# Skewing the attention bias with a repeated table in HBM instead of flip matmuls

## The reference

```
dist = qi + W - kj
bias = jnp.moveaxis(rel_bias[t5_bucket(dist * r)], -1, 0)
s = jnp.einsum('bnqchd,bnkchd->bnchqk', qb, kb).astype(jnp.float32) * (dh ** -0.5)
s = s + bias.astype(jnp.float32)
s = jnp.where(valid[None, :, None, None], s, -jnp.inf)
```

## Time and profile before

| | |
|---|---|
| median of three runs | 1124.41 us (1123.78 to 1126.25) |
| the profiled execution, its own time | 1126.25 us |
| its span, first to last instruction | 1124.4 us |
| TensorE matmul busy | 1025.4 us, 91% |
| VectorE busy | 859.4 us, 76% |
| ScalarE busy | 619.6 us, 55% |
| mean granted TensorE clock | 0.948 of full speed |

### The profile page before, as it was taken

The page is one execution under the profiler, slowest core; times in us unless marked ns, Lnnn a source line. Parts: engine busy times, 40 slices in busy tenths (PEclk is TensorE's granted clock), DMA queues, the critical chain, the costliest instruction groups (busy, mean ns, idle before and its releaser), DMA issues.

```text
span 1124.4 us, 13500 instructions
## 1 busy us (share of the span) xinstructions
PE 1025.4 (91%) x4842; PEld 851.0 (76%) x4842; DVE 859.4 (76%) x928; ACT 619.6 (55%) x535; POOL 95.9 (9%) x77
## 2 busy tenths in 40 slices
PE   4999999999999994789999999999999999999740
PEld 3788797978768784678888888888888888888630
DVE  3387838383855676679989999899999999999738
ACT  3223515153354233357777777777777777777622
POOL 3100000000000031000111101111011110111014
PEclk8999999999989995789999999999999999999965
DMA  9432212122132645479999999999999999999141
GB/s 287 116 105 76 75 38 75 38 76 75 75 112 75 230 177 231 166 278 356 367 367 363 361 381 368 359 357 374 380 373 360 356 376 370 384 365 346 39 174 75
DMA packets 71649, 268.67 MB, mean 239 GB/s; under 512 B 7412, under 2 KB 28920, under 8 KB 53696
## 3 DMA queue, kind: packets, MB, share of 16 engines
q1 hardware_dynamic: 64352, 252.72, 60.0%
q0 software_dynamic: 7264, 15.51, 3.9%
HBM read 264.83 MB, written 13.13 MB: 247 GB/s over the span
## 4 chain that ended last, share of the span: by engine, by line
PE 84%; DVE 8%; DMA 3%; ACT 3%; issue 2%; SPq 0%; DVEq 0%; POOLq 0%; ACTq 0%
PE ps L778 34%; PE ps L802 17%; PE ps L520 9%; PE ps L521 8%; PE ps L522 8%; PE ps L763 1%; PE ps L753 1%; DMA raw_m<-in_w_in 1%; PE ps L813 1%; PE ps L545 1%; DVE ot L1233 1%; DVE stats L1245 1%; PE ps L634 1%; PE ps L572 1%; ACT hi_m L844 1%
## 5 line engine op out<-in xcount | busy, mean ns | idle before, releaser
L1263 DVE TENSOR_TENSOR lo_m<-raw_e,hi_m 128x2048 fp32r<-128x2048 f32 x102 | 233.5, 2290 | 24.2 <-ACT hi_m L984 22.4
L984 ACT ACTIVATE hi_m<-raw_e 128x2048 fp32r<-128x2048 f32 x102 | 195.5, 1919 | 73.2 <-PE ps L778 48.7
L1263 DVE TENSOR_TENSOR lo_e<-raw_e,hi_e 128x2048 fp32r<-128x2048 f32 x51 | 117.1, 2296 | 15.0 <-ACT hi_e L984 13.3
L520 PE MATMUL ps<-xh,hi_m 128*128 128x512 f32 x288 | 116.5, 405 | 10.0 <-DVE lo_m L1065 10.0
L984 ACT ACTIVATE hi_e<-raw_e 128x2048 fp32r<-128x2048 f32 x51 | 97.8, 1919 | 35.1 <-PE ps L802 18.4
L1065 DVE TENSOR_TENSOR lo_m<-raw_m,hi_m 128x2048 fp32r<-128x2048 f32 x28 | 64.1, 2290 | 65.9 <-ACT hi_m L844 65.9
L521 PE MATMUL ps<-xl,hi_m 128*128 128x512 f32 x288 | 114.4, 397 | 0.0
L522 PE MATMUL ps<-xh,lo_m 128*128 128x512 f32 x288 | 113.9, 396 | 0.0
L778 PE MATMUL ps<-hi_m,xeh 128*128 128x512 f32 x344 | 95.0, 399 | 2.4 <-DVE xel L1405 2.4
L778 PE MATMUL ps<-hi_m,xel 128*128 128x512 f32 x344 | 93.1, 393 | 0.0
L778 PE MATMUL ps<-lo_m,xeh 128*128 128x512 f32 x344 | 93.0, 393 | 0.0
(11 more groups left out here) (260 smaller groups left out, 1918.5 us busy)
## 6 DMA issues: line engine op xcount, KB each, us to landing
raw_e<-in_expert_w_gate_up SPq DMA_DIRECT2D x85, 1024.0 KB, 7.0
raw_e<-in_expert_w_down SPq DMA_DIRECT2D x68, 1024.0 KB, 7.1
raw_m<-in_expert_w_gate_up SPq DMA_DIRECT2D x51, 1024.0 KB, 7.5
raw_m<-in_w_in SPq DMA_DIRECT2D x21, 1024.0 KB, 5.3
raw_m<-in_w_o SPq DMA_DIRECT2D x4, 1024.0 KB, 4.9
yt<-yd SPq DMA_DIRECT2D x4, 1024.0 KB, 7.9
xt<-in_x SPq DMA_DIRECT2D x4, 512.0 KB, 5.4
raw_m<-in_w_conv_out SPq DMA_DIRECT2D x2, 1024.0 KB, 5.0
```

The source lines that it names most:

```text
L520: pe.matmul(dst, a, c, start=first, stop=False)
L984: act.activation(hi_e[q % HE], raw_e[q % RE], ACT.Copy).then_inc(hi_ready, 1)
L1263: dve.tensor_tensor(lo_e[q % HE], raw_e[q % RE], hi_e[q % HE].bitcast(F32), ALU.subtract).then_inc(lo_ready, 1)
```

## The change

The table in HBM gets 128 copies of each of the 12 tables, one for each partition. With a pitch of 384 numbers for a row and a step of 383 from one partition to the next, the read itself runs backwards by one place per partition, so that it fills the bias tiles in the right order. `flip`, `skew`, the four matmuls and the four evictions go away. The write becomes three DMAs, one for each group, whose source names every row of `gsb` 128 times with a step of 0. The bias add of unit 0 waits for the six reads themselves.

```diff
-        gtab = nc.dram_tensor("gtab", [HPG, NG, GTW], F32).ap()
+        gtab = nc.dram_tensor("gtab", [NG * HPG, P, GTW], F32).ap()
...
-            pool.dma_start(flip, c_square[5]).then_inc(flip_in, 16)
...
             pool.wait_ge(gt_sb, NG)
-            pool.dma_start(gtab, gsb).then_inc(gt_out, 16)
-            pool.wait_ge(xT_done, KT)
-            pool.wait_ge(gt_out, 16)
+            for g in range(NG):
+                pool.dma_start(gtab[g * HPG:(g + 1) * HPG], bass.AP(gsb.tensor, gsb[:, g].offset,
+                               [list(gsb.ap[0]), [0, P], [1, GTW]])).then_inc(gt_out, 16)
+            pool.wait_ge(gt_out, 16 * NG)
             for a in range(2):
-                pool.dma_start(skew[:, a].rearrange("p (m c) -> p m c", m=2),
-                               bass.AP(gtab.tensor, a * NG * GTW, [[1, P], [2 * NG * GTW, 2], [1, 2 * P]])
-                               ).then_inc(skew_in, 16)
+                pool.dma_start(bm[:, a], bass.AP(gtab.tensor, a * P * GTW + P - 1,
+                                                     [[GTW - 1, P], [2 * P * GTW, 2], [1, 2 * P]])
+                               ).then_inc(bm_in, 16)
                 for g in (1, 2):
-                    pool.dma_start(skew[:, 1 + g, a * 2 * P:(a + 1) * 2 * P].rearrange("p (m c) -> p m c", m=2),
-                                   bass.AP(gtab.tensor, (a * NG + g) * GTW + P, [[1, P], [2 * NG * GTW, 2], [1, P]])
-                                   ).then_inc(skew_in, 16)
+                    pool.dma_start(bm12[:, g - 1, a], bass.AP(gtab.tensor, (HPG * g + a) * P * GTW + 2 * P - 1,
+                                                             [[GTW - 1, P], [2 * P * GTW, 2], [1, P]])).then_inc(bm_in, 16)
...
                 if u == 0:
-                    pe.wait_ge(bias_sb, 4)
+                    pe.wait_ge(glu_done, CT)
...
-                if s == 12:
-                    pe.wait_ge(glu_done, CT)
-                    pe.wait_ge(skew_in, 96)
-                    pe.wait_ge(flip_in, 16)
-                    for n in range(4):
-                        pe.matmul(ps[:, 2 + n], flip, skew[:, n], start=True, stop=True).then_inc(bias_mm, 1)
...
-                if s == 13:
-                    for a in range(2):
-                        act.wait_ge(bias_mm, a + 1)
-                        act.activation(bm[:, a], ps[:, 2 + a].rearrange("p (m c) -> p m c", m=2), ACT.Copy
-                                       ).then_inc(bias_sb, 1)
-                    for g in (1, 2):
-                        act.wait_ge(bias_mm, 2 + g)
-                        act.activation(bm12[:, g - 1], ps[:, 3 + g].rearrange("p (a m c) -> p a m c", a=2, m=2), ACT.Copy
-                                       ).then_inc(bias_sb, 1)
...
                 if u == 0:
-                    dve.wait_ge(bias_sb, 4)
+                    dve.wait_ge(bm_in, 96)
```

More of the change, by code:

```diff
@@ L169, in build @@
         csil = at("csil", [P, 2, S], F32, 128)
-        skew = at("skew", [P, 4, S], F32, 144)
         RAW_KB = (32, 40, 48, 160, 176.5, 144, 152, 0, 8, 16, 24, 184.5)
@@ L199, in build @@
         upper = tiny("upper", [P, P])
-        flip = tiny("flip", [P, P])
         ones = tiny("ones", [P, P])
@@ L263, in build @@
         xT_done, xh_ready, xl_ready = sem("xT_done"), sem("xh_ready"), sem("xl_ready")
-        gt_mm, gt_sb, gt_out, skew_in = sem("gt_mm"), sem("gt_sb"), sem("gt_out"), sem("skew_in")
-        flip_in, bias_mm, bias_sb = sem("flip_in"), sem("bias_mm"), sem("bias_sb")
+        gt_mm, gt_sb, gt_out, bm_in = sem("gt_mm"), sem("gt_sb"), sem("gt_out"), sem("bm_in")
         proj_done, proj_evac = sem("proj_done"), sem("proj_evac")
@@ L1476, in constants @@
 def constants():
-    sq = np.zeros((6, P, P), np.float32)
+    sq = np.zeros((5, P, P), np.float32)
     sq[0] = np.eye(P)
@@ L1492, in constants @@
         sq[4, r * 2 + m, a * HD:(a + 1) * HD] = 1.0
-    sq[5] = np.eye(P)[::-1]
     tb = np.zeros((NBUCKET + 1, NG, GTW), np.float32)
```

## The result

The changed kernel takes 1181.47 us (1180.31 to 1185.01) where the kernel before takes 1124.72 us in the same comparison: ratio 1.0511, with a 95% interval of 1.0493 to 1.053. It is 5.1% slower, +56.75 us. The forecast was slower too, but with +35.3 us. The time lies outside the forecast's own range (1156 to 1173) and inside that of rival C (1177.8, up to 1187). The profiled execution of the changed kernel has a span of 1180.4 us, 56.0 more than before.

A forecast was written before the change was run, and what follows sets the result against it. TensorE bounds the kernel until 108 us, then the line hangs on the first bias add. The 94.0 us table write delays that by 35.3 us, the 3.4 us saving lying inside the stall: 1124.41 + 35.3 = 1159.7 us, own range 1156 to 1173.

The forecast's parts named there:

- rival C: The table write also holds up the weight loads: chunk 5 lands at 134.3 us, +53.4 us, total 1177.8; chance 0.30.
- Slower, 0.85: Whole kernel: chance 0.85 that it gets slower by more than about 0.2%, 2.2 us.
- The write rate: Table write of 2.36 MB from four neighbouring partitions of gsb: 25.1 GB/s, 94.0 us, landing at 134.3 us.
- Rival B: The table write is hidden, the bias is in time and only -3.4 us remains: 1121.0 us; chance 0.13.
- D: The table write goes one stream at a time at 9 GB/s, 262 us: +203 us, 1328; chance 0.06.
- The bias: Bias tiles whole at 143.6 us, so the first bias add starts at about 143.7 instead of 108.38: +35.3 us.
- the loads: Weight loads beside the table write: no delay in the sum; TensorE still does step 14, to about 110.5 us.
- the credit of 3.4 us for the matmuls: Rival C's deduction for the four flip matmuls removed from TensorE, turning +56.8 us into +53.4.
- the slow restart: TensorE at half clock after standing idle: at most 2.5 us, put at 0 with 2.5 in the range.
- The removed work: Flip matmuls on TensorE -3.4 us if nothing else is late; ScalarE evictions, flip load and wait on transposes 0.
- the deadline: First bias add on VectorE: could start at 104.95 us without the flip matmuls, so the bias must be ready then.

The follow-up runs named there:

- the ladder: Five variants of the changed kernel whose table write reads different source partitions: 27 GB/s from 0 to 3, 52.6 or 97 from others, 342 from all 128.
- oneatatime: Changed kernel, but POOL waits for each of the three table writes before issuing the next; 1167.58 us, ratio 1.0365.
- before_plus: Kernel before, its bias in time, plus the slow 2.36 MB write behind its skewed reads into a tensor nobody reads; 1180.46 us, ratio 1.0491.
- spread128: Changed kernel, but tables made on all 128 partitions, each writing four of the copies; 1122.97 us, ratio 0.9972.
- ports4: Changed kernel, tables on 16 partitions, but the write reads only partitions 0, 4, 8 and 12; 1123.08 us, ratio 0.9972.
- hbmcopy: Changed kernel, but the 18 KB of tables go to HBM once and three HBM-to-HBM DMAs make the copies; 1123.32 us, ratio 0.9972.
- spread16: Changed kernel, but tables on 16 partitions, each writing 32 copies; 1122.58 us, ratio 0.9957; run again 1123.21 us, ratio 0.9982.

## Why the prediction was right or wrong

**Slower, 0.85: right.** The time lies in the range of 1128 to 1195, but above the forecast's own 1156 to 1173. The place, the table write, is right.

**The write rate: right, with luck.** 25.1 GB/s was read as a limit of the source, backed by 0.7 us of data; the real write had 25.5, and landed at 133.3 where 134.3 was forecast. The limit of the source is shown by the ladder. But the figure itself was the rate of one DMA engine in the output store, and no run shows why a source of four neighbours should have just that. With the 27.6 GB/s of the Trainium skill ("SBUF — State Buffer", section "Door 1: The DMA port swizzle (why `[64,N]` ≈ `[32,N]`)") the estimate was 85.5 us. By it the write would have been 7.1 us shorter than the measured 92.6. Rival B, one rate for each engine, is out: 11.4 engines moved no more than 3.9, and only a change of the partitions raised the rate. D is out with it.

**The bias: right in itself, but not last.** It was whole by 143.9 us at the latest, where 143.6 was forecast. oneatatime shows what that mechanism costs nearly alone: +41.1 us for a bias add 41.9 late. It came 6.6 us later than the forecast's: the writes, one after another, landed 9.1 us later, at 143.4, and the bias add followed 6.9 us behind them, where the forecast had 9.4.

**The failed step: the loads.** The sum had no term for them: it kept them out of the way of the write ("no weight load need be in flight") and let TensorE run on to 110.5 us ("can still do step 14"). In fact chunk 5 landed at 132.8 instead of 52.7, TensorE stopped at 82 us in front of step 10, and step 10 began 55.4 us late. The row that spoke against it stood in the profile, 10.0 against 5.3 us, and I made a rival of it with 0.30 instead of the forecast. What I held against it was that the engines might be only part occupied, or that the load might get three chunks through in 94 us. They were part occupied, 71%, and not one chunk was whole before 132.8 us. The reason is in the packets of 70 to 100 us: 1.7 of the write for each of the loads, 1.94 us each, so that a busy engine needs 3.3 us for one 1 KB packet of a load. A chunk is 1024 of them, 64 for each engine: 211 us, longer than the write, so that it becomes whole only when the write ends. This arithmetic is worked out and not tried by itself; that loads and not the bias set the time is shown by before_plus.

**Rival C's own numbers: nearly right.** Chunk 5 at 134.3, measured 132.8; step 10 +56.8, measured +55.4; total +53.4, measured +56.75 (56.0 between the two traces). The mis-sized term is the credit of 3.4 us for the matmuls: 0.6 came back, 1.7 went to the slow restart, for which the forecast had kept up to 2.5 us in its range and C nothing, and 1.1 to VectorE, which nobody had in a sum. The second slow stretch, 1.1 us, stood nowhere either. 53.4 - 1.4 + 2.9 + 1.1 is the 56.0.

**The removed work: right once the write is hidden.** With the write out of the way the same removal gives between -1.9 and -3.9 us in the five comparisons of spread128, ports4, hbmcopy and spread16, where B said -3.4, and the first bias add comes at 102.8 to 106.4, where 104.95 was the deadline.

## What to carry to other kernels

Price a DMA from a few partitions of SBUF by which partitions it reads, and never by its bytes over the core's rate: putting the same table on 16 partitions with one copy on VectorE turned +5.1% into -0.2 to -0.4%. A DMA whose source is slow isn't merely late itself; it holds the engines that it is spread over, so list every transfer that will be in flight beside it and ask when the first of them is needed. If it must be slow, issue it in pieces one after another: the rate is nearly the same (the whole landed 10 us later here), and the others keep their engines; +5.1% became +3.7%.

## What the runs showed of the hardware

- Three DMAs of four source rows each, in flight together, kept 11.4 engines busy; one at a time it was 3.9 engines, with the same 26 to 27 GB/s. The Trainium skill, "DMA: Bandwidth & Descriptors", "Rules for kernel authors", has at most four engines for an outermost count of four; the trace agrees for one DMA, and several add up.
- A load of 1 MB that took 5.3 us alone and 10.0 beside the skewed reads took 89.6 us beside a write of 27 GB/s, while the core's DMA moved 31 GB/s in all (70 to 100 us).
- A held load appears in the chain as "another core or an unknown queue"; the waits and the landing time give its name.
- TensorE, after standing idle for 54.8, 59.2 and 56.5 us, was granted 0.50 of full speed (the 1.2 GHz level) for its first 3.5, 5.5 and 3.9 us of work and then 1.00, and lost half of that time. Only the first of the three traces has a second slow stretch: 0.64 from 177 to 181 us, where TensorE was busy 3.20 of 4 us; it cost 1.1 us.
